# Statistics of the differential heads' norm in two rounded passes, with a remainder from GpSimd

## The reference

```python
    w = pm[:, 0] - lam * pm[:, 1]
    return jnp.einsum('bhqk,bkhe->bqhe', w.astype(v_all.dtype), v_all)
...
o = run_attention(core, (q,), is_prompt)
o = rms_norm(o, p['g_sub']) * (1.0 - lam_init)
om = memory_attn(qm, km, vm)
mix = jnp.concatenate([o.reshape(B, S, SELF_WIDTH), om.reshape(B, S, MEM_WIDTH)], axis=-1)
x = x + mix @ p['w_out']
```

## Time and profile before

| what | value |
|---|---|
| median of 3 runs | 1376.49 us (1375.23 to 1376.8) |
| time of the profiled execution | 1373.04 us |
| its span, first to last instruction | 1370.9 us |
| PE busy | 1300.1 us, 95% |
| POOL busy | 176.1 us, 13% |
| mean granted TensorE clock | 0.981 of full |
| squares `sqs` on ACT (L1030) | 6 instructions |
| statistics on PE (L674) | 12 instructions, two for each head |

### The profile page before, as it was taken

The page is one execution under the profiler, slowest core; times in us unless marked ns, Lnnn a source line. Parts: engine busy times, 40 slices in busy tenths (PEclk is TensorE's granted clock), DMA queues, the critical chain, the costliest instruction groups (busy, mean ns, idle before and its releaser), DMA issues.

```text
span 1370.9 us, 22151 instructions
## 1 busy us (share of the span) xinstructions
PE 1300.1 (95%) x8593; PEld 1264.3 (92%) x8593; DVE 749.6 (55%) x1152; ACT 566.9 (41%) x801; POOL 176.1 (13%) x195
## 2 busy tenths in 40 slices
PE   5799999999888999999999989999995999999999
PEld 5799999999876999999999989999994789999998
DVE  5665564454665565554455565554446646556533
ACT  6543343344344543433344333333343545334322
POOL 3400000045113100000131000000151430000000
PEclk9899999999999999999999999999997999999999
DMA  7544453443320344454454324454451014444343
GB/s 255 133 154 144 142 204 128 163 163 139 123 89 1 123 154 153 153 176 133 142 175 173 133 93 147 141 155 146 145 175 34 29 62 154 145 142 144 133 148 123
DMA packets 39064, 187.39 MB, mean 137 GB/s; under 512 B 4172, under 2 KB 14162, under 8 KB 23776
## 3 DMA queue, kind: packets, MB, share of 16 engines
q1 hardware_dynamic: 37824, 183.38, 39.2%
q0 software_dynamic: 1040, 3.13, 1.0%
q10 hardware_dynamic: 144, 0.11, 0.1%
HBM read 179.70 MB, written 6.90 MB: 136 GB/s over the span
## 4 chain that ended last, share of the span: by engine, by line
PE 84%; DVE 6%; ACT 4%; POOL 2%; issue 2%; DMA 1%; SPq 0%; ACTq 0%; DVEq 0%; POOLq 0%
PE bank L445 25%; PE bank L447 24%; PE bank L446 24%; ACT whi L862 2%; DVE wlo L1155 1%; PE bank L730 1%; PE bank L612 1%; PE bank L732 1%; PE bank L731 1%; DVE qz L1195 1%; PE bank L639 1%; POOL ew L1620 1%; PE bank L642 1%; POOL ssum L1575 1%; DMA memt<-in_memT 1%
## 5 line engine op out<-in xcount | busy, mean ns | idle before, releaser
L445 PE MATMUL bank<-xhi,whi 128*128 128x320 f32 (+1 forms) x1760 | 550.2, 313 | 23.2 <-DVE wlo L1155 12.2
L446 PE MATMUL bank<-xlo,whi 128*128 128x320 f32 (+1 forms) x1760 | 546.3, 310 | 0.0
L447 PE MATMUL bank<-xhi,wlo 128*128 128x320 f32 (+1 forms) x1760 | 546.2, 310 | 0.0
L1155 DVE TENSOR_TENSOR wlo<-raw,whi 128x2048 fp32r<-128x2048 f32 (+1 forms) x183 | 378.1, 2066 | 247.9 <-ACT whi L862 247.9
L862 ACT ACTIVATE whi<-raw 128x2048 fp32r<-128x2048 f32 (+1 forms) x183 | 315.4, 1723 | 246.0 <-PE bank L447 246.0
L445 PEld LDWEIGHTS bank<-xhi,whi 128*128 128x128 f32 x1760 | 333.8, 190 | 26.6 <-issue 14.8
L446 PEld LDWEIGHTS bank<-xlo,whi 128*128 128x128 f32 x1760 | 334.0, 190 | 0.5
L447 PEld LDWEIGHTS bank<-xhi,wlo 128*128 128x128 f32 x1760 | 333.7, 190 | 0.0
L445 PE MATMUL bank<-hhi,whi 128*128 128x320 f32 x704 | 219.4, 312 | 0.3 <-DVE wlo L1155 0.2
L447 PE MATMUL bank<-hhi,wlo 128*128 128x320 f32 x704 | 217.5, 309 | 0.0
L446 PE MATMUL bank<-hlo,whi 128*128 128x320 f32 x704 | 217.5, 309 | 0.0
(11 more groups left out here) (201 smaller groups left out, 1114.0 us busy)
## 6 DMA issues: line engine op xcount, KB each, us to landing
raw<-in_w_ffn_in SPq DMA_DIRECT2D x88, 1024.0 KB, 4.8
raw<-in_w_ffn_out SPq DMA_DIRECT2D x64, 704.0 KB, 4.1
raw<-in_w_in_a SPq DMA_DIRECT2D x10, 1024.0 KB, 4.8
raw<-in_w_out SPq DMA_DIRECT2D x8, 1024.0 KB, 4.8
raw<-in_w_kv SPq DMA_DIRECT2D x6, 1024.0 KB, 4.8
raw<-in_w_in_b SPq DMA_DIRECT2D x4, 1024.0 KB, 4.8
raw<-in_w_mkv SPq DMA_DIRECT2D x3, 1024.0 KB, 4.9
x<-in_xT SPq DMA_DIRECT2D x1, 1280.0 KB, 9.2
```

What stands on the lines that cost most here:

```text
L445: mm(acc, wh, mhi(ks[q]), start=start and q == 0, stop=False)
L446: mm(acc, wh, mlo(ks[q]), start=False, stop=False)
L447: last = mm(acc, wl, mhi(ks[q]), start=False, stop=stop and q == nk - 1)
L1155: tt(wlo[slot][:, 0:size], raw[slot][:, 0:size], f32(whi[slot][:, 0:size]), ALU.subtract).then_inc(lo_ready[slot], 1)
```

## The change

The six differential heads' statistics take the form of the other head norms. ACT writes the square rounded to fp32r into `hsq_hi`. POOL, at the place where `out_lo` returned at once, squares the tile in f32 (waiting for `o_taken`) and subtracts `hsq_hi` from it into `hsq_lo`. PE makes two fp32r passes in `head_stat` in place of one f32 matmul; the first waits for `hsq_ready`, the second for `hlo_ready`. The buffer `sqs` and two semaphores go; it lay beside `ew` under `xhi` and `xlo`, so no other buffer moves. The running numbers of the later norms rise by 6, which keeps each on its slot.

```diff
-HNORM = {... "sub": (4, 6, None), "kv": (5, 6, 18), "pb_q": (6, 6, 24), "pb_m": (7, 2, 30)}
+HNORM = {... "sub": (4, 6, 18), "kv": (5, 6, 24), "pb_q": (6, 6, 30), "pb_m": (7, 2, 36)}
...
-            sqs = sb("sqs", [P, 6, R], F32, region)
...
@@ PE, head_stat
-                sel = selq[:, 14 - 2 * j:142 - 2 * j]
+                sel = selo[:, 15 - j:143 - j] if hn == "sub" else selq[:, 14 - 2 * j:142 - 2 * j]
...
@@ PE, attention
-                def sub_stats(t):
-                    if t == 0:
-                        pe.wait_ge(hr_ready, HNORM["sub"][0])
-                    pe.wait_ge(sub_square, t + 1)
-                    mm(HS[:, 0:R], selo[:, 15 - t:143 - t].bitcast(F32), sqs[:, t, :], start=t == 0, stop=t == 5
-                       ).then_inc(sub_stat, 1)
...
                     if layer == 0 and 1 <= i <= 6:
-                        sub_stats(i - 1)
+                        head_stat("sub", i - 1, R)
...
@@ ACT, head_root
-                if hn == "sub":
-                    act.wait_ge(sub_stat, s_n)
-                else:
+                if hn != "sub":
                     nc.scalar.preload_act_table_set("natural_log_exp_and_others")
-                    act.wait_ge(hstat, s0 + s_n)
+                act.wait_ge(hstat, s0 + s_n)
...
@@ ACT, attention, out_hi
-                        nc.scalar.activation(sqs[:, t, :], out_tile_of(t), ACT.Square).then_inc(sub_square, 1)
+                        head_square("sub", t, out_tile_of(t), R)
...
@@ POOL, attention, out_lo
                     if unit["kind"] == "diff":
+                        head_squares_lo("sub", lambda j: out_tile_of(t), R, o_taken, lambda j: u + 1, [t])
                         return
```

More of the change, by code:

```diff
@@ L73 @@
 NORM = {"mkv0": 0, "in0": 1, "pa": 2, "in1": 3, "kv": 4, "pb": 5, "in3": 6}
-HNORM = {"mkv0": (0, 2, 0), "mkv1": (1, 2, 2), "pa_q": (2, 6, 4), "pa_k": (3, 8, 10), "sub": (4, 6, None),
-         "kv": (5, 6, 18), "pb_q": (6, 6, 24), "pb_m": (7, 2, 30)}
+HNORM = {"mkv0": (0, 2, 0), "mkv1": (1, 2, 2), "pa_q": (2, 6, 4), "pa_k": (3, 8, 10), "sub": (4, 6, 18),
+         "kv": (5, 6, 24), "pb_q": (6, 6, 30), "pb_m": (7, 2, 36)}
 AUX0 = {"mkv0": 0}
@@ L303, in encoder_kernel @@
         mix_lo = sem("mix_lo")
-        sub_square = sem("sub_square")
-        sub_stat = sem("sub_stat")
         sub_row = sem("sub_row")
```

## The result

The kernel after takes 1385.65 us (median of six runs; before 1376.49). One of the six took 2137.38 us at a mean granted clock of 0.569; the other five lie between 1382.54 and 1386.63 us, and their median is 1385.32. The ratio of the kernel after to the kernel before is 1.0063, with a 95% interval of 1.005 to 1.0077, and 1.0075 (1.0061 to 1.0088) when both were run again: 9 to 11 us slower. The forecast was 1387.2. The profiled execution took 1386.63 us, span 1384.8, which is 13.9 us over the span before. The two profiles already stand 2.6 us apart at the start of unit 1's turns, ahead of every changed instruction (398.76 against 396.19). Nearly all of that is time at a lower granted clock ahead of the change: from 345.5 to 348.8 us and from 389.8 to 393.2 us it is 0.50 in the profile after and 1.00 in the one before.

The account below looks back on a forecast made before the run. PE was taken to bound attention of layer 0 in units 1 to 6; 5.6 us of waits, 2.7 us of tail and 2.4 us of clock on 1376.5 gave 1387.2 us, range 1381.5 to 1391.5.

Parts of the forecast that it names:

- The place of the wait: Attention of layer 0: POOL's square and subtraction stand behind the next unit's normalise; PE's second pass starts at T + 5.88.
- POOL's work hides: Rival: POOL's remainder is ready before PE asks, so the kernel gets 1.5 to 1.7 us faster; chance 0.04 (1374.9 us).
- The term behind the forecast: PE's statistic per head: two fp32r passes cost 0.30 us where the f32 pair takes 0.59, saving 0.29 us.
- The price of a wait: Units 1 to 5: PE's delay is paid in every unit, none caught up; 5.6 us up to unit 6.
- POOL's length from both sides: POOL's square and subtraction: 1.68 us a head as lower bound, taken; upper bound 1.79 us more beside DVE's split.
- The tail: From unit 6, T being its turns' start: head 5's late remainder delays ACT's root and values(7) by 2.7 us.
- The clock in unit 7: Clock falls to 1.2 GHz in unit 6's long gap, lengthening values(7): 2.4 us, bounds 0 and 4.5.
- The clock in units 1 to 5: PE's gaps of 1.3 us in units 1 to 5 cost no clock: nothing added.
- The sum: Whole kernel: 8.3 us of waits plus 2.4 us of clock on the median 1376.5 us give 1387.2 us.
- the clock holds: Rival: the same waits without the 2.4 us of clock, +8.3 us; chance 0.32 (1384.8 us).

Follow-up runs that it names:

- filled kernel: The kernel after with PE's waits for the six remainders filled by passes over a selector of zeros: 1383.12 us, ratio 1.0058 to the kernel before.
- POOL's load alone: The kernel before with two squares a head added on POOL at the place of the change, for which PE never waits: 1375.77 us, ratio 0.9998.
- the squares first: The kernel after with POOL's square and remainder put ahead of the wait for the next unit's reciprocals: 1373.31 us, ratio 0.9981 to the kernel before.
- the kernel without the square: The kernel after with POOL's square left out for the six differential heads, the remainder being the tile less itself: 1379.31 us, ratio 1.0027.

## Why the prediction was right, and where it was not

- **The place of the wait: right.** PE waits for POOL's subtraction, which stands behind `dg`. Moved ahead of the reciprocals, as the rival "POOL's work hides" asked, it costs nothing: the experiment made that rival true and the time went to the other side, as it said, by 2.6 us in the timings where it forecast 1.5 to 1.7. The trace shows only 0.9 us of that between the turns of unit 1 and those of unit 6. The term behind the forecast was too large: the two passes take 0.38 us (407.55 to 407.93), not 0.30, and a unit of 5.07 us shrinks to 4.83, so a head saves 0.24 us, not 0.29, and less in units 4 and 5 (4.23 against 4.29, 5.02 against 5.15).
- **The price of a wait: right.** Forecast 6.06 (three times), 5.42 and 6.76 us from turn to turn. The filled kernel, without clock losses, shows 6.16, 6.09, 6.09, 5.45 and 6.80. From unit 1 to unit 6 that is 30.59 us against 24.73: 5.9 us where 5.6 were forecast. POOL's three pieces came as priced.
- **POOL's length from both sides: right at the lower bound.** No subtraction in attention of layer 0 took longer than 0.87 us in the kernel after, or 0.89 in the filled one; none was stretched as the one of 2.68 us in the earlier trace rows was.
- **The tail: right in its waits.** `values(7)` was to move from T + 6.85 to T + 9.6. It starts at T + 9.73 in the kernel after and T + 9.68 in the filled one, and the root on ACT at T + 6.69 (438.02) where T + 6.55 was forecast.
- **The clock in unit 7: right in kind, in the place, and too dear.** It fell at the end of the long wait for head 5. From `values(7)` to `wo0` the kernel after takes 9.11 us, where the kernel before takes 7.45: 1.7 us, forecast 2.4. In the filled kernel, where head 5's wait is not empty, the clock did not fall there.
- **The clock in units 1 to 5: wrong.** The step that failed is the one that put the clock's cost in units 1 to 5 at nothing: the prediction takes from the Trainium skill, page "TensorE: Matmul & The Clock Gate", section "HAM oscillation — how this bites in real kernels", that only a long wait costs, and that therefore "the gaps of 1.3 us in units 1 to 5 don't". The traces here don't bear that reading out, and they decide. In the profile after, unit 2 lost 0.5 us by it (6.59 against 6.09) and unit 5 lost 1.6 us (8.35 against 6.80); in the second profile unit 3 lost 1.0 us (7.09). The rows of before had no stretch with gaps of that length, repeated, and I took the absence of a row for a zero.
- **The sum.** 8.3 us of waits and 2.4 of clock were forecast, 10.7 together. In the timings the filled kernel is 7.7 us over the kernel before, and the kernel after 10.6 on that chip and 9.2 in the first timing. In the traces, from the turns of unit 1 to `wo0`, the kernel after is 12.4 and 11.3 us over the kernel before. Of these 8.7 are waits, as the filled kernel shows (5.9 up to unit 6, and 2.8 from there to `values(7)`, 9.68 against 6.85); most of the other 3.7 and 2.6 us is time under the low clock. Part of the loss comes back behind `wo0`: the second profile of the kernel after and the one with POOL's load alone start unit 1 at 398.52 and 398.53, and stand 11.3 us apart at `wo0` and 10.4 at the end of their spans. So the shift at `wo0` is in the total but for 1 us, and what brings that back stays open. The waits are thus some 8 to 9 us and the clock 1 to 4. The forecast of the time is good to 1 or 2 us, and partly by luck: a tail loss forecast too large stood beside losses in earlier units that were not forecast, and beside a gain behind `wo0` that was not forecast either.

The rival "the clock holds" (1384.8) is refuted by the profiles, though its time lies nearer to the measured 1385.65 than the forecast does. A time alone would not have told them apart.

## What to carry to other kernels

Work given to an idle engine is as late as its place in that engine's program, not as the data it needs: POOL was idle for 3.1 to 4.7 us ahead of the reciprocals in units 1 to 5, and the tile had been there for most of a unit, but the work stood behind a wait for something later. (With the squares first, POOL waits for ACT's rounded square until T + 2.84, 405.94 less 403.10; that is still early enough.) Before handing a step over, find the first wait ahead of it in the new engine's order and ask whether the step fits in front of it (here that turned 9 to 11 us lost into 2.6 us won, of which the trace shows 0.9 at the place of the change), or else let the consumer take the result one round later.

## What the hardware showed beyond that

Waits of PE of 1.0 to 1.6 us in nearly every unit of 6 us were followed by a fall of the granted clock now and then, at another unit in each profile, while one wait of 1.66 us was not. Each such fall cost 0.5 to 1.7 us on top. On GpSimd an f32 product or difference of 128x320 elements took 0.72 us when both inputs were the same tile and 0.86 us when they were two tiles, with an fp32r output too (0.72 in the kernel without the square). Filling the waits with passes over zeros kept the granted clock at 1.00 for 38.5 us, and with 58 more passes on PE the median was 2.9 us lower, with intervals that overlap. Two profiles of kernels with the same code up to there can start attention of layer 0 more than 2 us apart (391.61 before, 393.94 in the kernel with POOL's load alone; 1.4 of these 2.3 us come with a fall of the clock, which was 1.00 in the one and 0.50 in the other from 347.4 to 350.6 us), so a difference of spans should be cut at a common instruction ahead of the change.
